# The last expert pair of a mixture-of-experts layer, written out behind its loop

## What is computed

```python
def expert(acc, e):
    wu, bu, wd, bd, cw = e
    y = clamped_swiglu(t @ wu + bu) @ wd + bd
    return acc + cw[:, None] * y, None
out, _ = lax.scan(expert, zeros_like(t), (w_up, b_up, w_down, b_down, combine.T))
...
x = x + gt2 * moe_ffn(h, ...)      # gt2: one row for the prompt, one row per decode token
y = rmsnorm(x, g_final)
```

## Time and profile before

| | us |
|---|---|
| median of three runs | 1199.84 |
| lowest and highest run | 1198.00, 1200.22 |
| the profiled execution, its own time | 1199.41 |
| its span, first to last instruction | 1197.6 |

### The profile page before, as it was taken

How to read it: one execution, slowest core, us unless ns; L and a number is a source line. 1 busy time by engine, 2 the same in 40 slices (tenths; PEclk the granted TensorE clock), 3 DMA queues, 4 the chain that set the end, 5 groups by cost and what they waited for, 6 DMA issues and landing times.

```text
span 1197.6 us, 14207 instructions
## 1 busy us (share of the span) xinstructions
PE 1127.2 (94%) x5487; PEld 455.7 (38%) x5487; DVE 352.5 (29%) x756; ACT 175.2 (15%) x322; POOL 53.4 (4%) x81
## 2 busy tenths in 40 slices
PE   6999999999999999989898989898989898999995
PEld 3777756633233333323232323232323232323231
DVE  1645277332313212121212121212122222222224
ACT  2331171301010101010101010101010101010102
POOL 3400001100000000000000000000000000000000
PEclk9999999999999999999999999999999999999998
DMA  9971299689999999999999999999999999999992
GB/s 362 362 255 71 76 376 361 274 288 405 431 432 431 431 430 431 431 431 431 432 429 432 431 431 431 430 432 431 431 430 432 431 431 432 430 432 431 432 430 103
DMA packets 46880, 462.00 MB, mean 386 GB/s; under 512 B 6529, under 2 KB 9793, under 8 KB 19162
## 3 DMA queue, kind: packets, MB, share of 16 engines
q1 hardware_dynamic: 39890, 444.16, 88.4%
q0 software_dynamic: 5712, 13.62, 3.2%
q10 hardware_dynamic: 1256, 3.92, 0.9%
HBM read 461.28 MB, written 5.78 MB: 390 GB/s over the span
## 4 chain that ended last, share of the span: by engine, by line
PE 69%; DMA 27%; DVE 3%; issue 1%; ACT 1%; SPq 0%; ACTq 0%; DVEq 0%
PE bank L1436 35%; DMA ring<-in_w_up 23%; PE bank L1329 6%; PE bank L1429 5%; PE bank L1457 4%; PE bank L824 3%; PE bank L925 3%; PE bank L902 2%; PE bank L1242 2%; DMA arena<-in_w_down 2%; PE bank L848 1%; PE bank L998 1%; PE bank L1335 1%; PE bank L982 1%; DMA x<-in_x_sample 1%
## 5 line engine op out<-in xcount | busy, mean ns | idle before, releaser
L1436 PE MATMUL bank<-ring,arena 128*64 128x512 f32 x1536 | 362.9, 604 | 16.7 <-DMA ring<-in_w_up 14.5
L1436 PEld LDWEIGHTS bank<-ring,arena 128*64 128x64 f32 x1536 | 98.0, 137 | 258.2 <-issue 214.1
L1457 PE MATMUL bank<-arena 128*64 128x512 f32 x512 | 115.5, 595 | 14.2 <-DMA arena<-in_w_down 14.2
L1457 PE MATMUL bank<-ring,arena 128*64 128x512 f32 x512 | 116.1, 595 | 0.0
L1436 PE MATMUL bank<-arena 128*64 128x512 f32 x512 | 116.1, 595 | 0.0
L1977 DVE TENSOR_SCALAR arena<-bank 128x256 f32<-128x256 f32 x64 | 24.2, 419 | 290.6 <-PE bank L1436 290.6
L1329 PE MATMUL bank<-arena,mods 128*128 128x512 f32 (+2 forms) x204 | 94.4, 629 | 0.0
L788 ACT ACTIVATE arena<-arena 128x512 f32<-128x512 f32 x32 | 20.2, 631 | 501.0 <-DVE arena L1977 501.0
L1967 DVE TENSOR_TENSOR x<-x,bank 128x512 f32<-128x512 f32 x64 | 44.0, 687 | 146.6 <-PE bank L1329 146.6
L1995 DVE COPY arena<-bank 64x512 f32<-64x512 f32 x32 | 22.0, 688 | 177.0 <-PE bank L1457 177.0
L1457 PEld LDWEIGHTS bank<-arena 128*64 128x64 f32 x512 | 35.4, 137 | 91.6 <-issue 65.8
(11 more groups left out here) (319 smaller groups left out, 823.2 us busy)
## 6 DMA issues: line engine op xcount, KB each, us to landing
ring<-in_w_up SPq DMA_DIRECT2D x96, 2048.0 KB, 23.8
arena<-in_w_up SPq DMA_DIRECT2D x32, 2048.0 KB, 25.2
ring<-in_w_down SPq DMA_DIRECT2D x32, 2048.0 KB, 22.3
arena<-in_w_down SPq DMA_DIRECT2D x32, 2048.0 KB, 23.4
ring<-in_w_ada SPq DMA_DIRECT2D x24, 1024.0 KB, 12.5
ring<-in_w_in SPq DMA_DIRECT2D x4, 2048.0 KB, 21.7
ring<-in_w_in SPq DMA_DIRECT2D x3, 1024.0 KB, 13.2
arena<-in_state_hgrn POOLq DMA_DIRECT2D x8, 256.0 KB, 10.2
```

Of the source, the lines that this page charges most:

```text
L1436: mm = pe.matmul(B[2 * e + c % 2][64 * a:64 * a + 64, :], lhsT=xTe[:, k, 64 * e:64 * e + 64], rhs=big(n)[:, CH * r + 512 * c:CH * r + 512 ...
L1457: mm = pe.matmul(B[4 + e][64 * a:64 * a + 64, :], lhsT=gT[e].rearrange("p (j a t) -> p j a t", j=4, a=2)[:, k % 4, k // 4, :], rhs=big(n). ...
```

## The change

The loop runs once less: `npass` now holds passes x 16 - 1, read into `ahead`, and each engine writes out one more turn behind its loop, `pair_steps(ahead, True)`. In it:

- nothing is done for a next pair (no row selection, row numbers, gather, turning, copies), and SP's `If` is gone from its loop;
- the outputs are gated from PSUM straight into `ysg` (semaphore `half_gated`), instead of copied and then gated; ACT keeps both halves in `ysb` for the decode tokens (`y_kept`, `y_crossed`);
- PE combines prompt block 0, the decode tokens, then prompt block 1; the four identity products are gone.

The decode tokens stay in two strips of 32 partitions by 512 columns up to the end: their gate row (`gate_st`), final weights (`g_st`) and residual are loaded or stored in strips, `moe_s` is gated and added to the residual during the last pair (`wst`), and the two half sums of squares are added by two small products with a new constant, `strips`. The result is stored by two transfers.

```diff
-                  ("same", NB), ("heads", NB * HH), ("spread", 64)):
+                  ("same", NB), ("heads", NB * HH), ("spread", 64), ("strips", 32)):
...
+    put("strips", r[:, None] % 32 == np.arange(32)[None, :])
... SP
+            ahead = sp.value_load(npass[0:1, 0:1], min_val=PAIRS - 1, max_val=MAXPASS * PAIRS - 1)
...
+            with sp.Fori(0, ahead) as it:
+                other_chunks(it)
+                for c in range(BIGS):
+                    sp.wait_ge(chunks_used, it * PER + (PRE + PER + c - BIGS + 1))
+                    expert_chunk(c, (it + 1) % PAIRS)
+            other_chunks(ahead)
...
-            sp.dma_start(O["ys"].rearrange("b s d -> (b s) d"), x[0:NB, 2, :]).then_inc(sem("result_stored"), 16)
+            for a in range(2):
+                sp.dma_start(O["ys"].rearrange("b s d -> (b s) d")[:, 512 * a:512 * (a + 1)],
+                             x[32 * a:32 * a + NB, 2, 0:512]).then_inc(sem("result_stored"), 16)
... POOL
-            pool.dma_start(gate2s[0:NB, :], mod_dram[1:1 + NB, :]).then_inc(sem("gate_s_full"), 16)
+            pool.memset(gate_st, 0.0).then_inc(sem("gate_s_cleared"), 1)
+            pool.wait_ge(sem("gate_s_cleared"), 1)
+            for a in range(2):
+                pool.dma_start(gate_st[32 * a:32 * a + NB, :], mod_dram[1:1 + NB, 512 * a:512 * (a + 1)]).then_inc(sem("gate_s_full"), 16)
...
+            pool.wait_ge(sem("xT_made"), 2)
+            for a in range(2):
+                pool.dma_start(g_st[32 * a:32 * a + NB, :], wide(A["g_final"].rearrange("(a n) -> a n", a=1)[:, 512 * a:512 * (a + 1)], 0, NB)).then_inc(sem("g_fin_full"), 16)
... ACT
-                    act.activation(ysb[r, e, :], B[4 + e][r, :], ACT.Copy).then_inc(sem("y_copied_a"), 1)
+                    act.activation(ysb[r, e, :], B[4 + e][r, :], ACT.Copy).then_inc(sem("y_kept" if last else "y_copied_a"), 1)
+                    if last:
+                        other = slice(64 * (1 - e), 64 * (1 - e) + 64)
+                        act.wait_ge(sem("half_gated"), 2 * e + 1)
+                        act.activation(ysb[r, 1 - e, :], B[4 + e][other, :], ACT.Copy).then_inc(sem("y_crossed"), 1)
...
+            act.wait_ge(sem("v_ready"), 1)
+            act.activation(junk_s[0:64, :], vst[0:64, :], ACT.Square, accum_out=ssum3[0:64, :]).then_inc(sem("sums"), 1)
+            act.wait_ge(sem("v_mean"), 1)
+            act.activation(root3[0:64, 2:3], B[4][0:64, 0:1], ACT.Sqrt, scale=1.0 / D, bias=eps[0:64, :]).then_inc(sem("roots"), 1)
... PE
+                def combine_tokens(t):
+                    for a in range(2):
+                        pe.wait_ge(sem("half_gated"), 3 + a)
+                        combine(B[2 * t + a][:, :], slice(P * t, P * (t + 1)), ysg[:, a, :]).then_inc(sem("x2_made"), 1)
+
+                def combine_decode():
+                    pe.wait_ge(sem("y_kept"), 2)
+                    pe.wait_ge(sem("y_crossed"), 2)
+                    for a in range(2):
+                        mm = combine(B[6][32 * a:32 * a + 32, :], slice(S, S + 32), ysb[:, a, :])
+                    mm.then_inc(sem("decode_made"), 1)
...
+                if last:
+                    pe.wait_ge(sem("u_read"), it * 2 + 3)
+                    combine_tokens(0)
+                    combine_decode()
+                    combine_tokens(1)
...
+            pe.wait_ge(sem("sums"), 1)
             for a in range(2):
-                pe.matmul(B[6 + a][0:NB, :], lhsT=ident[:, 32 * a:32 * a + NB], rhs=moe_s, start=True, stop=False,
-                          skip_group_check=True)
...
+                mm = pe.matmul(B[4][32 * a:32 * a + 32, 0:1], lhsT=C("strips", slice(0, 64)), rhs=ssum3[0:64, :], start=True, stop=True,
+                               skip_group_check=True)
+            mm.then_inc(sem("v_mean"), 1)
... DVE
-            dve.tensor_copy(npass[:, :], csum[0:1, :]).then_inc(sem("npass_ready"), 1)
+            dve.tensor_scalar(npass[:, :], csum[0:1, :], float(PAIRS), -1.0, ALU.mult, ALU.add).then_inc(sem("npass_ready"), 1)
...
+                    for e in range(2):
+                        dve.wait_ge(chunks_used, it * PER + (PRE + 2 * UPS + DOWNS * (e + 1)))
+                        other, own = slice(64 * (1 - e), 64 * (1 - e) + 64), slice(64 * e, 64 * e + 64)
+                        dve.tensor_tensor(ysg[own, 1 - e, :], B[4 + e][other, :], gate2[other, 512 * (1 - e):512 * (2 - e)], ALU.mult).then_inc(sem("half_gated"), 1)
+                        dve.wait_ge(sem("y_kept"), e + 1)
+                        dve.tensor_tensor(ysg[own, e, :], B[4 + e][own, :], gate2[own, 512 * e:512 * (e + 1)], ALU.mult).then_inc(sem("half_gated"), 1)
+                        if e == 0:
+                            dve.wait_ge(sem("gate_s_full"), 32)
+                            dve.wait_ge(sem("sum_added"), it * 5 + 6)
+                            link(dve.tensor_tensor(wst[0:64, :], moe_s[0:64, :], gate_st[0:64, :], ALU.mult))
+                            dve.tensor_tensor(wst[0:64, :], wst[0:64, :], x[0:64, 2, 0:512], ALU.add).then_inc(sem("w_ready"), 1)
...
+            add_share(0, 0)
+            add_share(0, 1)
+            dve.wait_ge(sem("decode_made"), 1)
+            dve.wait_ge(sem("w_ready"), 1)
+            link(dve.tensor_tensor(vst[0:64, :], B[6][0:64, :], gate_st[0:64, :], ALU.mult))
+            dve.tensor_tensor(vst[0:64, :], vst[0:64, :], wst[0:64, :], ALU.add).then_inc(sem("v_ready"), 1)
+            add_share(1, 0)
             half_mean_of(0)
+            add_share(1, 1)
+            final_norm(0)
             half_mean_of(1)
-            final_norm(0)
             final_norm(1)
...
+            dve.scalar_tensor_tensor(out=x[0:64, 2, 0:512], in0=vst[0:64, :], scalar=root3[0:64, 2:3], in1=g_st[0:64, :],
                                      op0=ALU.mult, op1=ALU.mult).then_inc(sem("result"), 1)
```

More of the change, by code:

```diff
@@ L784, in _, with pair_steps @@
             count_from_one(act, "y_copied_a", "gT_copied")
-            with act.Fori(0, total) as it:
+            def pair_steps(it, last):
                 for e in range(2):
@@ L791, in _ @@
                         act.activation(Wc[:, 0:NTOK], B[4][:, 0:NTOK], ACT.Copy).then_inc(sem("wc_copied"), 1)
-                    if e:
+                    if e and not last:
                         copy_rows(it * 2 + 4)
@@ L1371, in _, with pair_steps @@
             count_from_one(pe, "gT_made")
-            with pe.Fori(0, total) as it:
+            def pair_steps(it, last):
                 def chunk_landed(c):
@@ L1417, in _ @@
                             turn_weights()
-                            find_rows(it + 2)
+                            if not last:
+                                find_rows(it + 2)
                         if e and k == 4:
@@ L1444, in _ @@
                         pe.wait_ge(sem("wc_copied"), it + 2)
-                    else:
+                    elif not last:
                         pe.wait_ge(sem("idx_ready"), it + 1)
@@ L1462, in _ @@
                             mm.then_inc(chunks_used, 1)
[L1464 to L1467, removed]
[L1468 to L1478 removed]
+                if last:
[3 more added lines that the diff above has]
+                    combine_tokens(1)
+            with pe.Fori(0, ahead) as it:
+                pair_steps(it, False)
+            pair_steps(ahead, True)
+            pe.wait_ge(sem("sums"), 1)
+            for a in range(2):
+                mm = pe.matmul(B[4][32 * a:32 * a + 32, 0:1], lhsT=C("strips", slice(0, 64)), rhs=ssum3[0:64, :], start=True, stop=True,
+                               skip_group_check=True)
+            mm.then_inc(sem("v_mean"), 1)
         @block.vector
@@ L1950, in _, with pair_steps @@
                 wait_emptied(dve, name)
-            with dve.Fori(0, total) as it:
+            def pair_steps(it, last):
                 pair = bass.ds((it % PAIRS) * 2, 2)
@@ L1996, in _ @@
[L1996 to L2004, removed]
+                if not last:
+                    own_rows(after).then_inc(sem("own_row_ready"), 1)
+                    copy_rows(it * 2 + 3)
+                    for e in range(2):
+                        dve.wait_ge(chunks_used, it * PER + (PRE + 2 * UPS + DOWNS * (e + 1)))
+                        src, dst = slice(64 * (1 - e), 64 * (1 - e) + 64), slice(64 * e, 64 * e + 64)
+                        dve.tensor_copy(ysb[dst, 1 - e, :], B[4 + e][src, :]).then_inc(sem("y_copied_d"), 1)
+                    dve.wait_ge(sem("y_copied_a"), it * 2 + 3)
+                    dve.wait_ge(sem("y_copied_d"), it * 2 + 3)
+                    gate_outputs()
+                else:
+                    for e in range(2):
+                        dve.wait_ge(chunks_used, it * PER + (PRE + 2 * UPS + DOWNS * (e + 1)))
+                        other, own = slice(64 * (1 - e), 64 * (1 - e) + 64), slice(64 * e, 64 * e + 64)
[7 more added lines that the diff above has]
```

(4 more changed lines are left out.)

80 lines of the change are left out of this document (33 added, 47 removed).

## The result

| | us |
|---|---|
| before, median of 20 runs (lowest, highest) | 1199.47 (1197.69, 1202.03) |
| after, median of 20 runs (lowest, highest) | 1203.24 (1200.52, 1206.02) |
| ratio after to before, 95% interval | 1.0028 (1.0020 to 1.0036) |
| the profiled execution of after: its time, its span | 1202.22, 1200.4 |

One run of after took 2289.09 us and one of a later kernel 3977.95 us, and the ranges and ratios here leave them out. The change makes the kernel 3.4 us slower (0.28%), where 4.3 us of gain were forecast. The time lies outside the forecast's range.

A forecast was written before the change was run, and what follows sets the result against it. The weight stream was taken as the bound, PE close behind; -0.1 before the loop, -4.55 at the end and +0.34 for stores gave -4.3 us, from 1199.84 to 1195.5, range 1193.5 to 1198.2.

The forecast's parts named there:

- The change, before the loop: Before the loop: the loop-count read gains 0.1 us; POOL's memset, small transfers and 32 more constant columns cost 0.
- rival 1: Last pair: one or two instruction packets delay the last chunk by 1.1 or 2.1 us, 1196.6 or 1197.6; chance 0.10.
- Reading the loop count, -0.1: Before the loop: a 0.22 us register step on DVE may go, -0.22 to +0.2, taken as -0.1 us.
- Dropped work of the last pair: 0: Last pair: PE loses 2.0 us of work, worth nothing because it only waits longer for weight chunks.
- (a): After the last chunk's products: gating straight from PSUM without identity products starts `combine` at 1180.0 instead of 1181.03.
- (b): Prompt block 0 at the end: its adds start near 1181.1 and 1182.0.
- (c): Decode tokens ahead of prompt block 1 spend some 0.8 of 1.0 us gained; second scaling ends at 1189.4, -0.2 us.
- (d): Behind the norms: decode work hides under the second scaling; result ready near 1190.5 instead of 1195.05, -4.55 us including earlier end steps.
- (e): Final store: the result leaves in two issues, the second 0.34 us later, +0.34 us.
- Rival 2: Written-out last pair: PE stalls 10.2 us for an instruction packet, slack takes 3.0, giving 1202.7; chance 0.06.
- Rival 3: Last chunk's products: TensorE's clock falls to 1.2 GHz, doubling their 3.65 us, giving 1199.2; chance 0.05.
- Rival 4: At the end: a decode-token step holds up DVE, so the end moves less than 2.4 us; chance 0.03.

The follow-up runs named there:

- experiment 5: Changed kernel with tiles in old places (1193.21): next-pair work kept in last pair, 1193.72; decode tokens combined last, 1195.76; copies back ahead of gating, 1194.96.

## Why the prediction failed, step by step

**The step that failed** is in "The change, before the loop": "The 32 columns more in the constants are 16 KB: 0." I priced the transfer of these columns, and that is nothing indeed (the wider tensor alone: 0.9997). I didn't look at what lies behind the tile that holds them. Moving it by these 128 bytes costs some 7 us on the kernel before and 9.6 us on the changed one, more than all that the end could give; some 6 us of it are seen in the packets of the loop (611.0 to 615.1 ns each). The bound itself was read rightly: by the earlier trace rows the stream is the limit, so whatever makes a packet slower is paid in full, over 900 us. That reading should have led to the question of what the change does to each of the weight transfers, where I only asked what it adds to their number (rival 1).

The Trainium skill, DMA: Bandwidth & Descriptors, How a descriptor splits into AXI transactions, has a rule that bears on it: the first transaction of a descriptor that does not start on a 256-byte boundary starts at the boundary below, and the bytes ahead of the descriptor's start cost beats as well. The page tells it of reads; for the place that is written it states nothing. If it held there too, 16 KB that start 128 bytes behind a boundary would take 516 beats of 32 bytes instead of 512, by this page 0.8% as an estimate; 615.1 for 611.0 ns is 0.7%. In the detail the runs part from such a count. By it (4 beats for 128 bytes, 2 for 64, 3 for 96, and so on, also estimates) the mean over the six buffers would be 1.0 beat more in the kernel before, 2.3 with the arena moved, 2.7 with four off, and 3.0, 3.7 and 5.0 in those moved by 64, with the ring moved and with the wider tile. The packets keep this order (611.0, 611.2, 612.4, 614.9, 614.9 and 615.0 ns), but not the sizes: the first two steps give next to nothing, the step from 2.7 to 3.0 gives most of the loss, and from 3.0 to 5.0 little comes.

**Point by point.**

- *What bounds the kernel*: held, see above.
- *Reading the loop count, -0.1*: did not come. The step of 0.22 is still there, in the chain of after:

```profile
248.19 0.22 DVEq L1964
```

- *POOL's memset and small transfers, SP's `If`: 0*: nothing in the trace speaks against it; no run has it alone.
- *Dropped work of the last pair: 0*: held; with the work kept the last chunk comes no later (experiment 5). PE did only 42.31 us of work in the 43.5 us of the last pair, where it had 43.13, and the end of the stream set the end of the pair all the same:

```profile
1134.50:1178.00 43.50, 42.31 (x181) 12.78 (x181) 9.03 (x17) 2.85 (x5) 0.00 (x0) 1.00 1.01 427
```

- *(a) Gating*: held. `combine` starts 0.86 us behind the last product (1187.26 to 1188.12); it was 1.82. Forecast was a gain of 1.03, it came as 0.96. The form that was not in the trace, a product of 64x512 from PSUM, takes the 0.68 that the copy took. The rows of the end, to which the points below refer too:

```profile
1187.28 0.68 DVE L2037 TENSOR_TENSOR arena<-bank,arena 64x512 f32<-64x512 f32 x1 [6.31 <-PE bank L1492]
...
1195.90 1.42 DVE L2059 SCALAR_TENSOR_TENSOR x<-x,small,arena 128x512 f32<-128x512 f32 x2
...
1196.34 0.23 PE L1510 MATMUL bank<-small,const 64*32 64x1 f32 x4 [3.37 <-ACT arena L832]
1196.61 0.26 ACT L834 ACTIVATE small<-bank,small 64x1 f32<-64x1 f32 x1 [0.33 <-PE bank L1510]
...
1198.19 0.67 SPq L479 DMA_DIRECT2D out_ys<-x  x2
```

- *(b), (c) The norms*: held. The second scaling ends at 1197.32 (1195.90 + 1.42), 10.06 behind the last product; before it was 10.41, forecast 10.2.
- *(d) The decode tokens' end*: right in its mechanism, mis-sized by 0.4. The result is ready at 1198.16 (1197.42 + 0.74 in the chain of after), 10.90 behind the last product; before it was 15.84 (1195.05), so -4.94 for -4.55. The `strips` products took 0.23 and not 0.6. I had leaned on the clock of 0.84 in the last microseconds of before; in this place of after the clock is 1.00, though PE waited 3.37 us ahead of them:

```profile
1195.00:1197.50 2.50, 0.23 (x4) 0.14 (x4) 2.07 (x7) 1.16 (x4) 0.00 (x0) 1.00 0.56 210
```

  So the root is ready at 1196.87, 0.45 ahead of the second scaling's end, and not with it.
- *(e) The stores, +0.34*: wrong in sign. From the result to the span's end it is 2.24 us (1198.16 to 1200.4), where it was 2.55 (1195.05 to 1197.6): -0.3. The two issues take 0.67 together, but what follows the second is shorter than what followed the one of before.
- *The sum behind the last chunk*: -4.2 forecast, -5.2 in the trace. The changed kernel in its right place gains 6.1 us by its ratio (4.3 to 7.9 by its interval); its 1193.62 lies at the lower end of the range.
- *Rival 1, instruction packets*: they came, three in the last pair, and cost nothing that the trace shows (the queues q8 and q14 in 1120 to 1201 us: packets, MB, share):

```profile
q8 instruction: 2, 0.03, 0.2%
q14 instruction: 1, 0.01, 0.0%
```

- *Rival 2, a code stall*: did not happen; PE works through the last pair as above. The time came out near its 1202.7, by chance: the last products start as late in the kernel before with nothing but the wider tile, which has no new code (its chain):

```profile
1183.96 3.65 PE bank L1457 x16
```

- *Rival 3, the clock*: stayed at 1.00 in the last pair and up to the result. It was 0.54 in 1198 to 1199 us and 0.50 behind that, where PE has no work left.
- *Rival 4*: the change does what it says, behind the loop.

The range failed since every case in it took the 900 us of stream as given; my only mechanism on the slower side was a stall.

## What to carry to other kernels

Where a stream of transfers is the bound, a change must be asked what it does to each transfer, and a tile that grows by a few bytes moves every tile declared behind it: write down the start of the large buffers before and after, modulo 256. Put large stream buffers first, or pad small tiles, so that their place doesn't hang on a constant's width. What such a place costs was measured here for one stream of 16 KB packets in one kernel, and the cost of a start depended on where the other buffers lay. And when an edit whose mechanism is in the trace brings no gain, compare the bytes moved in the same window before looking at the edited place: here 428 for 431 GB/s named the cause's place at once, while nothing around the edit was wrong.

## What the runs showed of the hardware

- The 16 KB packets of the weight stream take some 0.7% longer when all six destination buffers start off a multiple of 256 bytes in their partition: 614.9 to 615.1 ns on average for 611.0, 428 GB/s for 431, 6 us in 826 us of stream, 7 to 10 us of 1200 in the times. 64, 96, 128, 160 and 224 bytes off occur in these kernels; moving by 256 is free.
- It does not add up by buffers: with two of six off the packets take 611.0 to 611.2 ns and the times don't change, with four 612.4 ns and 2 us. Why is open.
- The loss does not shrink with PE's reads of the buffers: it is 8.9 us with half of the expert products.
- The transfer share of 1.01 and a busy PE look alike at 428 and at 431 GB/s. Only bytes per time tell them apart.
- A last store of two small transfers ended the span 0.3 us sooner behind the result than a single one that moved the same bytes: 2.24 us with 16 rows of 2 KB after, 2.55 with 8 rows of 4 KB before.
